# Hybrid attention and DeltaNet layer on one core: inverse's transposed copy moved to VectorE, beginning reordered

## The chip, the cores and the metric

The kernel runs on one core of one Trainium2 chip. The metric is the device time of one execution in microseconds (us). Less is better. The kernel before took 1398.04 us as the median of 3 runs (1397.48 to 1400.84).

## What is computed

One layer of a hybrid decoder, in fp32, for a prompt of 512 tokens and a sample group of 8 sequences with one token each (520 token columns), width 2048. After an RMSNorm, one input projection gives all columns of two mixers, and one output projection (2048 x 2048) ends the layer, with a second RMSNorm and the residual.

```python
h = rmsnorm(x, g_pre); p = h @ w_in          # 8208 columns: q,k,v,z of A; q,k,v of B, z of B; beta, a
# mixer A: 8 heads x 128, dilated windows (128,1), (512,4), (2048,16), partial rotary on 32 dims
# mixer B: gated DeltaNet, 8 heads x 128; conv of width 4, SiLU, l2 norms, chunks
a_mat = where(strict, (kbeta @ k.T) * decay, 0)
t_mat = triangular_solve(a_mat + eye, eye)   # the inverse U of this text, per chunk and head
u = t_mat @ (v * beta);  w = t_mat @ (kbeta * exp(gcum))
# then a recurrence over the chunks with a 128x128 state per head
y = x + rmsnorm(concat(o_a * silu(z_a), o_b * silu(z_b)) @ w_out, g_post)
```

The caches, the conv rows and the states are outputs too. The kernel uses chunks of 128 tokens where the reference has 64; the result is the same.

## The kernel before, in words

The five engines run hand-written streams that meet in semaphores. The activations are kept transposed (model dimension on the partitions, tokens on the free axis) and every projection operand is split into a high part (`h_hi`, `w_hi`) and a remainder (`h_lo`, `w_lo`), both fp32r, so that three matmuls at fp32r speed stand for one fp32 product. For each output tile of 128 columns, 16 blocks of the model dimension times 3 matmuls are needed, for each of two halves of the 520 tokens (`HALF` = 260): 96 matmuls in 8 *segments* of 12 (`segment`, L521 to L539, the matmuls on L532 to L534; a segment is one half and one quarter q of the model dimension). Each half has a PSUM bank of `PJ`.

**Tiles.** Tile T = 0 holds the 16 columns of beta and a (`w_ba`), tiles 1 to 64 the 8 columns groups of each of the 8 heads, then 16 tiles of the output projection. SP loads the weights of tile T + 1 in four quarters, ScalarE copies each to `w_hi` (`hi`, L885), VectorE and GpSimd form `w_lo` (L1266, L1733), all while TensorE works on tile T.

**The order of the other work.** All work of the two mixers is woven into the projection: each engine has generators (`own_b`, `own_a`, `mix_b`, `delta_decode`, `tail_a`, `attn_decode`, `gates`), and `step(work)` advances each of them to its next `yield` after every segment. So a head's stretch of 8 tiles has 64 steps, and which operation stands behind which in an engine's queue follows from the steps and from the order of the generators in the list: `own_a` stands ahead of `mix_b`, and `mix_b` ahead of `delta_decode`.

**The inverse.** `mix_b` forms for each chunk of 128 tokens the inverse U (`b_U`) of a unit triangular matrix by doubling. There are 7 levels; at level n the blocks of size 2^n are joined. GpSimd multiplies the matrix by a mask for the level (L1786) and makes the first U (L1791). For n = 1 to 6: TensorE multiplies the mask's block by the transposed copy T (`b_T`) (Y, L705), ScalarE copies Y to SBUF (L1135), TensorE multiplies Y by U (Z, L715) and, for n = 1 to 5, U by Y (L720); VectorE subtracts Z from U (L1492) and L720's product from T (L1495) and clears part of Y (L1496). The first T is made by four transposes on TensorE (L694) and a copy on ScalarE (L1131). Between L705 and L715, and between L720 and the next L705, TensorE runs one segment:

```python
for n in range(1, LEVELS):
    yield
    ...
    pe.wait_ge(s["mix_UT"], UTS * h + 3 * (n - 1) - 1)
```

In the same steps VectorE has the rope of mixer A (`rope_on`, L1353 to L1355) and the additions into the decode state (L1578, behind TensorE's outer product L775), the two small operations L1570 and L1571 ahead of them.

**The beginning.** SP loads the samples, chunk 0 of the prompt, the norm's weights, the identity, chunk 1, small state rows, chunks 2 and 3, the 16 columns of small weights, constants, then tile 1. ScalarE squares each chunk (L961) and takes the inverse root (L890, L891), VectorE scales (`x_scale`, L1292), TensorE transposes (state rows L556, samples L560, chunks L571), ScalarE and VectorE split into high and low (`x_hi` L969, `x_lo` L1299). When all 4 chunks and the samples are split, TensorE starts tile 0.

Of the kernel before, what the change touches and what calls it, by code (L numbers as in the profile page):

```python
# [12 lines left out]
P = 128  # L13
# [4 lines left out]
HALF = TT // 2  # L18
# [49 lines left out]
def layout(x):  # L68
# [5 lines left out]
         "w_ba": w[:, 64 * P:].reshape(NQ, 4, P, 16).transpose(0, 2, 1, 3),  # L74
# [9 lines left out]
class Chain:  # L84
# [73 lines left out]
def build(nc, x_prompt, x_sample, cache_k, cache_v, state_conv, state_delta, g_pre, w_in, w_ba, conv_w, a_log, dt_bias,  # L158
# [7 lines left out]
    with ExitStack() as ctx:  # L166
# [43 lines left out]
        s_in = sz[:, 0:P]  # L210
        xba = cq[0:16, :]
# [30 lines left out]
        vecT = sb("vecT", [P, KT + 1])  # L242
# [41 lines left out]

        def all_blocks(x, n, odd):
            return x.rearrange("p c (k a s) -> p (c k) a s", a=2, s=1 << n)[:, :, odd, :]

        def mx(n):
# [4 lines left out]
            "c_in g_in consts s_loaded x_sq rstd_ok x_scaled hT_ps h_hi_ok h_lo_ok st_ps st_sb memset_ok "  # L293
# [13 lines left out]
            "mix_kk mix_qk mix_A mix_QK mix_B mix_U0 mix_T_ps mix_T mix_Y_ps mix_Y mix_Z mix_UT ch_kS ch_r "  # L307
# [26 lines left out]
        def _(sp):  # L334
# [16 lines left out]
            sp.dma_start(xin[:, 1, :], x_prompt[0, P:2 * P, :]).then_inc(x_in[1], 16)  # L351
            sp.dma_start(scin[0:24], state_conv[0].rearrange("b i c -> (b i) c")).then_inc(s["c_in"], 16)
# [3 lines left out]
            for c in range(2, NC):  # L356
                sp.dma_start(xin[:, c, :], x_prompt[0, c * P:(c + 1) * P, :]).then_inc(x_in[c], 16)
# [14 lines left out]
            for q in range(NQ):  # L372
                wait_lo(0, q)
                load_w(w_in, tile_of(0, 0), q)
            sp.wait_ge(s["x_sq"], NC + 1)
# [145 lines left out]
        def _(pe):  # L521
            def segment(T, par, half, q, first=False):
# [3 lines left out]
                if q == 0 and not first:  # L526
                    pe.wait_ge(s["proj_sb"], 2 * T - 1 + half)
                tok = slice(half * HALF, (half + 1) * HALF)
                out = PJ[:, half, 0:HALF]
# [16 lines left out]
            def stretch(h, work):  # L546
                for j in range(NT):
                    project(NT * h + (T_H + j), (1 + j) % 2, work)
                over(work)


            pe.wait_ge(s["c_in"], 80)
            pe.transpose(MD[:, 0, 0:KT + 1], s_in[0:KT + 1], ident[0:KT + 1, 0:KT + 1]).then_inc(s["st_ps"], 1)
            for m in range(3 * NH):
                bank, o = m // 12, (m % 12) * 28
# [1309 lines left out]
```

## Time and profile before

| what | value |
|---|---|
| median of 3 runs | 1398.04 us |
| profiled execution, its own time | 1396.91 us |
| span of the profile | 1395.1 us |
| mean granted TensorE clock | 0.975 of full speed |
| TensorE busy | 1313.8 us (94%) |
| VectorE, ScalarE, GpSimd busy | 785.9, 535.7, 338.4 us |

The profile shows one execution, taken by the hardware profiler; an engine's row gives start, duration, source line, operation, operands and, in brackets, how long the engine sat idle before it and who released it. PEld is TensorE's weight load. Matmuls are pipelined, so the durations of neighbours overlap; the distance of their starts is what one costs.

### The profile page before, as it was taken

To read this page: it belongs to the slowest core of one execution; us is meant where nothing else is said; L and a number is where in the kernel's file an instruction comes from. 1 tells how busy PE (TensorE), PEld (TensorE's weight loads), DVE (VectorE), ACT (ScalarE), POOL (GpSimd) and SP (SyncE) were. 2 spreads that over 40 slices of the span, in tenths; PEclk is the share of its full clock that TensorE was granted. 3 is DMA by queue.
4 is the path that set the end of the run, shared out by engine and by line. 5 is a ranking of instruction groups with operands and counts; after the bars stand their busy time and mean duration, and the time that the engine had idled before them with its cause. 6 is when DMAs were issued, how large, how long until landed. Compare 5 with 4: busy or idle time off the path is not lost.

```text
span 1395.1 us, 29226 instructions
## 1 busy us (share of the span) xinstructions
PE 1313.8 (94%) x10446; PEld 1265.7 (91%) x10446; DVE 785.9 (56%) x1873; ACT 535.7 (38%) x1447; POOL 338.4 (24%) x287
## 2 busy tenths in 40 slices
PE   4999999999999999999999899989998998989997
PEld 3998998999899988998999899989998997989996
DVE  6366366636763676367636763676267635474445
ACT  6243346224633363246323633363236325512210
POOL 0224212421242124212421242124212411212220
PEclk9999999999999999999999999999999999989999
DMA  5332324233423342324133423342334233422253
GB/s 185 114 104 72 107 87 152 71 99 95 152 71 94 100 152 71 96 98 152 71 94 100 152 71 92 102 147 76 91 103 156 81 107 133 144 70 89 94 184 126
DMA packets 84638, 151.81 MB, mean 109 GB/s; under 512 B 10873, under 2 KB 29266, under 8 KB 82962
## 3 DMA queue, kind: packets, MB, share of 16 engines
q1 hardware_dynamic: 74158, 144.87, 32.3%
q10 hardware_dynamic: 10384, 5.50, 1.4%
q8 instruction: 81, 1.33, 0.4%
q14 instruction: 15, 0.12, 0.0%
HBM read 132.19 MB, written 17.27 MB: 107 GB/s over the span
## 4 chain that ended last, share of the span: by engine, by line
PE 69%; DVE 15%; issue 7%; ACT 6%; DMA 1%; POOL 1%; ACTq 0%; SPq 0%; DVEq 0%; POOLq 0%
PE PJ L532 15%; PE PJ L533 15%; PE PJ L534 15%; PE MX L705 3%; PE MX L715 2%; DVE memx L1416 2%; PE MX L720 2%; DVE memx L1427 2%; ACT kv L1183 1%; PE MD L757 1%; ACT w_hi L885 1%; PE MX L637 1%; PE MX L617 1%; DVE kv L1592 1%; PE MD L775 1%
## 5 line engine op out<-in xcount | busy, mean ns | idle before, releaser
L532 PE MATMUL PJ<-h_hi,w_hi 128*128 128x260 f32 x2432 | 725.4, 298 | 3.0 <-DVE w_lo L1266 1.6
L533 PE MATMUL PJ<-h_lo,w_hi 128*128 128x260 f32 x2432 | 694.4, 286 | 0.0
L534 PE MATMUL PJ<-h_hi,w_lo 128*128 128x260 f32 x2432 | 692.9, 285 | 0.0
L532 PEld LDWEIGHTS PJ<-h_hi,w_hi 128*128 128x128 f32 x2432 | 466.2, 192 | 21.1 <-issue 8.9
L533 PEld LDWEIGHTS PJ<-h_lo,w_hi 128*128 128x128 f32 x2432 | 465.9, 192 | 2.8 <-issue 1.7
L534 PEld LDWEIGHTS PJ<-h_hi,w_lo 128*128 128x128 f32 x2432 | 465.2, 191 | 0.0
L1733 POOL TENSOR_TENSOR w_lo<-w_raw,w_hi 128x512 fp32r<-128x512 f32 (+1 forms) x162 | 214.2, 1322 | 941.4 <-ACT w_hi L885 941.4
L885 ACT ACTIVATE w_hi<-w_raw 128x512 fp32r<-128x512 f32 (+1 forms) x324 | 199.0, 619 | 103.9 <-PE PJ L534 81.1
L1266 DVE TENSOR_TENSOR w_lo<-w_raw,w_hi 128x512 fp32r<-128x512 f32 (+1 forms) x162 | 116.1, 723 | 164.8 <-ACT w_hi L885 160.1
L1135 ACT ACTIVATE mem<-MX 128x256 f32<-128x256 f32 x48 | 18.6, 389 | 215.3 <-PE MX L705 215.3
L1786 POOL TENSOR_TENSOR mem<-mem,levels 128x512 f32<-128x512 f32 x56 | 71.8, 1293 | 33.8 <-DVE mem L1474 33.8
L1492 DVE TENSOR_TENSOR mem<-mem,MX 128x256 f32<-128x256 f32 x48 | 20.1, 418 | 85.5 <-PE MX L720 72.3
L1416 DVE SCALAR_TENSOR_TENSOR memx<-memx,cw 128x512 f32<-128x512 f32 x72 | 60.8, 844 | 1.7
L912 ACT ACTIVATE memx<-PJ 128x260 f32<-128x260 f32 (+1 forms) x130 | 49.4, 380 | 23.3 <-PE PJ L534 20.9
L818 PE MATMUL PJ<-h_hi,w_hi 128*128 128x260 f32 x160 | 50.1, 313 | 7.1 <-DVE h_lo L1642 3.0
L705 PE MATMUL MX<-mem 128*128 128x64 f32 x384 | 48.8, 270 | 6.8 <-DVE mem L1495 6.8
L705 PEld LDWEIGHTS MX<-mem 128*128 128x128 f32 x384 | 46.9, 191 | 8.4 <-DVE mem L1495 7.3
L1592 DVE CUSTOM_DVE_ANT_0 kv<-kv,qb 128x128 f32<-128x128 f32 x192 | 52.2, 329 | 0.0
L715 PE MATMUL MX<-mem 128*128 128x64 f32 x384 | 48.0, 268 | 0.0
L819 PE MATMUL PJ<-h_lo,w_hi 128*128 128x260 f32 x160 | 47.3, 295 | 0.0
L820 PE MATMUL PJ<-h_hi,w_lo 128*128 128x260 f32 x160 | 47.1, 295 | 0.0
L715 PEld LDWEIGHTS MX<-mem 128*128 128x128 f32 x384 | 47.0, 191 | 0.0
(306 smaller groups left out, 1671.3 us busy)
## 6 DMA issues: line engine op xcount, KB each, us to landing
w_raw<-in_w_in SPq DMA_DIRECT2D x256, 256.0 KB, 2.6
w_raw<-in_w_out SPq DMA_DIRECT2D x64, 256.0 KB, 2.8
kv<-in_cache_win_k SPq DMA_DIRECT2D x24, 512.0 KB, 3.4
kv<-in_cache_win_v SPq DMA_DIRECT2D x16, 512.0 KB, 4.1
mem<-in_x_prompt SPq DMA_DIRECT2D x4, 1024.0 KB, 10.9
S<-in_state_delta SPq DMA_DIRECT2D x8, 512.0 KB, 3.4
out<-S SPq DMA_DIRECT2D x8, 512.0 KB, 3.8
out<-mem ACTq DMA_DIRECT2D x16, 256.0 KB, 2.3
```

What stands on the lines that cost most here:

```text
L532: pe.matmul(out, wh, h_hi[:, k, tok], start=k == 0, stop=False)
L533: pe.matmul(out, wh, h_lo[:, k, tok], start=False, stop=False)
L534: last = pe.matmul(out, wl, h_hi[:, k, tok], start=False, stop=k == KT - 1)
L705: last = pe.matmul(blocks(mx(1)[:, c, :], n, 0), b_B[n % 2][:, c, :], blocks(b_T[:, c, :], n, 0), start=True, stop=True)
L715: last = pe.matmul(blocks(mx(2)[:, c, :], n, 1), b_Y[:, c, :], blocks(b_U[:, c, :], n, 1), start=True, stop=True)
L818: pe.matmul(out, wh, h_hi[:, k, tok], start=start and i == 0, stop=False)
L885: act.activation(w_hi[:, par, 4 * q:4 * q + 4, 0:n], w_raw[:, q, :, 0:n], ACT.Copy).then_inc(s["w_hi_ok"], 1)
L1266: dve.tensor_tensor(w_lo[:, par, 4 * q:4 * q + 4, 0:n], w_raw[:, q, :, 0:n], w_hi[:, par, 4 * q:4 * q + 4, 0:n].bitcast(F32), ALU.subtract ...
L1416: link(dve.scalar_tensor_tensor(acc[:, 0:TP], xq[:, i:i + TP], w[:, 24 + i:25 + i], acc[:, 0:TP], ALU.mult, ALU.add))
L1592: last = dve.tensor_tensor_reduce(out=x, in0=x, in1=qb[:, b * HD:(b + 1) * HD], scale=1.0, scalar=0.0, op0=ALU.mult, op1=ALU.add, accum_ou ...
L1733: pool.tensor_tensor(w_lo[:, par, 4 * q:4 * q + 4, 0:n], w_raw[:, q, :, 0:n], w_hi[:, par, 4 * q:4 * q + 4, 0:n].bitcast(F32), ALU.subtrac ...
L1786: ins = pool.tensor_tensor(b_B[n % 2], b_A, levels[:, n, :].unsqueeze(1).to_broadcast((P, NC, P)), ALU.mult)
```

## The change

1. *Transposed copy.* TensorE's first transposes (L694), ScalarE's copy (L1131) and, at levels 1 to 4, L720 and L1495 are gone. VectorE instead transposes U as a whole, 128x512, in blocks of 32x32, once behind U's making (in the step of L1482) and once behind each L1492 of the levels 1 to 4. At level 5 L720 and L1495 stay.
2. *Halves.* The two token halves are 256 and 264 columns wide instead of 260 and 260, in all tiles.
3. *Beginning.* The DMAs are issued in another order, the small weights come in one load with another layout, tile 1's weights ahead of chunks 2 and 3, the samples and the state rows behind them. The first half (chunks 0 and 1) of tiles 0 and 1 is projected first, with the transposes of the constants, of chunk 2, of the samples and of chunk 3 between the segments, then the second half of both. The samples are scaled by the norm's weights behind their transposes instead of ahead.

```diff
-HALF = TT // 2
+SPLIT = 2 * (TP // 4)
+TOKENS = (slice(0, SPLIT), slice(SPLIT, TT))
+WIDTH = (SPLIT, TT - SPLIT)
+def bank(T, half):
+    return T if isinstance(T, int) and T < 2 else half
+def made(T, half):
+    return 2 * half + T + 1 if isinstance(T, int) and T < 2 else 2 * T + half + 1
...
@@ sync: order of the loads @@
-            sp.dma_start(xs_in, x_sample.rearrange("b t d -> (b t) d")).then_inc(x_in[NC], 16)
-            sp.dma_start(xin[:, 0, :], x_prompt[0, 0:P, :]).then_inc(x_in[0], 16)
             for n in range(2):
                 sp.dma_start(g_bc[n], g_pre[0, n * WA:(n + 1) * WA].partition_broadcast(P)).then_inc(s["g_in"], 16)
-            sp.dma_start(ident[:], c_ident).then_inc(s["c_in"], 16)
+            sp.dma_start(xin[:, 0, :], x_prompt[0, 0:P, :]).then_inc(x_in[0], 16)
+            sp.dma_start(ident[:], c_ident).then_inc(s["ba_in"], 16)
+            sp.dma_start(ba_raw, w_ba).then_inc(s["ba_in"], 16)
             sp.dma_start(xin[:, 1, :], x_prompt[0, P:2 * P, :]).then_inc(x_in[1], 16)
+            for q in range(NQ):
+                load_w(w_in, tile_of(0, 0), q)
+            for c in range(2, NC):
+                sp.dma_start(xin[:, c, :], x_prompt[0, c * P:(c + 1) * P, :]).then_inc(x_in[c], 16)
+            sp.dma_start(xs_in, x_sample.rearrange("b t d -> (b t) d")).then_inc(x_in[NC], 16)
...
-            for q in range(NQ):
-                sp.dma_start(w_raw[:, q, :, 0:16], w_ba[q]).then_inc(raw_in[q], 16)
...
@@ tensor @@
+            def first_tiles():
+                after = {(0, 1): const_transposes, (0, 3): lambda: x_transposes(2), (1, 1): sample_transposes,
+                         (1, 3): lambda: x_transposes(3)}
+                for half in range(2):
+                    for T in range(2):
+                        for q in range(NQ):
+                            if half == 1 and T == 0:
+                                pe.wait_ge(s["h_lo_ok"], 4 * NC - 3 + q + 1)
+                            elif T == 0:
+                                pe.wait_ge(s["h_lo_ok"], 4 + q + 1)
...
+                            if half == 0 and (T, q) in after:
+                                after[T, q]()
...
-                pe.wait_ge(s["mix_U0"], h + 1)
-                for c in chunks:
-                    last = pe.transpose(mx(0)[:, c, :], b_U[:, c, :], ident[:])
-                last.then_inc(s["mix_T_ps"], 1)
...
-                    if n < LEVELS - 1:
+                    if n == LEVELS - 2:
                         for c in chunks:
                             last = pe.matmul(blocks(mx(3)[:, c, :], n, 0), b_U[:, c, :],
                                              blocks(b_Y[:, c, :], n, 0), start=True, stop=True)
...
@@ scalar: the beginning, and the copy @@
+            x_rstd(0, 0)
+            x_rstd(1, 1)
+            ba_hi()
+            x_rstd(2, 2)
+            x_hi(0)
+            x_hi(1)
+            x_rstd(3, 3)
+            for q in range(NQ):
+                hi(1, 1, q, first=True)
+            x_rstd(4, NC)
...
-                act.wait_ge(s["mix_T_ps"], h + 1)
-                act.activation(b_T, mx(0), ACT.Copy).then_inc(s["mix_T"], 1)
...
@@ vector: mix_b @@
                 dve.tensor_tensor(sz, xz, ez, ALU.mult).then_inc(s["z_ok_b"], 1)
+                dve.wait_ge(s["mix_U0"], h + 1)
+                dve.transpose(flat(b_T), flat(b_U)).then_inc(s["mix_T"], 1)
                 yield
                 for n in range(1, LEVELS):
                     yield
                     yield
-                    z = (2 * LEVELS - 3) * h + 2 * (n - 1) + 1
-                    dve.wait_ge(s["mix_Z"], z)
-                    if n < LEVELS - 1:
-                        dve.wait_ge(s["mix_Z"], z + 1)
+                    dve.wait_ge(s["mix_Z"], LEVELS * h + n + n // (LEVELS - 2))
                     u = all_blocks(b_U, n, 1)
                     dve.tensor_tensor(u, u, all_blocks(mx(2), n, 1), ALU.subtract).then_inc(s["mix_UT"], 1)
-                    if n < LEVELS - 1:
+                    if n < LEVELS - 2:
+                        dve.wait_ge(s["mix_UT"], UTS * h + 3 * n - 2)
+                        dve.transpose(flat(b_T), flat(b_U)).then_inc(s["mix_UT"], 1)
+                    elif n == LEVELS - 2:
                         t = all_blocks(b_T, n, 0)
                         dve.tensor_tensor(t, t, all_blocks(mx(3), n, 0), ALU.subtract).then_inc(s["mix_UT"], 1)
```

## Rows read from the trace of the kernel before

**Rows 1.** The page, busy time by engine and the chain that ended last.
```profile
PE 1313.8 (94%) x10446; PEld 1265.7 (91%) x10446; DVE 785.9 (56%) x1873; ACT 535.7 (38%) x1447; POOL 338.4 (24%) x287
...
PE 69%; DVE 15%; issue 7%; ACT 6%; DMA 1%; POOL 1%; ACTq 0%; SPq 0%; DVEq 0%; POOLq 0%
```

**Rows 2.** TensorE by line: count, busy us, mean ns of one, idle before.
```profile
L720 PE MATMUL MX<-mem 128*128 128x64 f32 x320 | 42.3, 275 | 0.0
...
L694 PE MATMUL MX<-ident,mem 128*128 128x128 f32 x32 | 4.9, 276 | 1.4 <-POOL mem L1791 1.4
```

**Rows 3.** Timeline of TensorE, third head: start us, us, what, idle before.
```profile
400.22 0.60 PE L694 MATMUL MX<-ident,mem 128*128 128x128 f32 x4
...
405.63 1.00 PE L715 MATMUL MX<-mem 128*128 128x64 f32 x8
406.46 1.06 PE L720 MATMUL MX<-mem 128*128 128x64 f32 x8
...
408.86 1.00 PE L705 MATMUL MX<-mem 128*128 128x64 f32 x8
409.79 1.12 PE L775 MATMUL MD<-rb 8*128 8x512 f32 x2
...
416.59 1.10 PE L705 MATMUL MX<-mem 128*128 128x64 f32 x8 [0.83 <-DVE mem L1495]
```

**Rows 4.** Timeline of VectorE, the same stretch.
```profile
400.10 1.00 DVE L1571 SCALAR_TENSOR_TENSOR gS<-dd,vecT,memx 128x8 f32 x1
...
407.56 0.42 DVE L1492 TENSOR_TENSOR mem<-mem,MX 128x256 f32<-128x256 f32 x1 [1.60 <-PE MX L720]
...
411.55 1.16 DVE L1353 TENSOR_TENSOR memx<-memx,memr 32x520 f32<-32x520 f32 x1
...
414.32 1.56 DVE L1355 TENSOR_TENSOR memx<-memx,memr 32x520 f32<-32x520 f32 x1
415.81 0.40 DVE L1492 TENSOR_TENSOR mem<-mem,MX 128x256 f32<-128x256 f32 x1
...
433.01 0.62 DVE L1353 TENSOR_TENSOR memx<-memx,memr 32x520 f32<-32x520 f32 x1
```

**Rows 5.** Timeline of GpSimd, the same stretch.
```profile
399.92 1.16 POOL L1786 TENSOR_TENSOR mem<-mem,levels 128x512 f32<-128x512 f32 x1
...
412.12 3.20 POOL L1786 TENSOR_TENSOR mem<-mem,levels 128x512 f32<-128x512 f32 x2
...
425.51 2.29 POOL L1786 TENSOR_TENSOR mem<-mem,levels 128x512 f32<-128x512 f32 x2
```

**Rows 6.** TensorE waits: releaser, total us, times, longest.
```profile
PE MX L705 <- DVE mem L1495: 6.8, 8, 0.9
```

**Rows 7.** Beginning: timelines of ScalarE, VectorE and TensorE.
```profile
17.50 1.91 ACT L961 ACTIVATE memr<-mem 128x2048 f32<-128x2048 f32 x1 [2.19 <-DMA mem<-in_x_prompt]
...
26.66 2.04 ACT L969 ACTIVATE h_hi<-MX 128x512 fp32r<-128x512 f32 x4
...
21.87 0.69 DVE L1299 TENSOR_TENSOR h_lo<-MX,h_hi 128x512 fp32r<-128x512 f32 x1 [0.65 <-ACT h_hi L969]
...
15.75 2.74 PE L556 MATMUL MX<-ident,memx 28*128 28x28 f32 x24
...
37.81 0.56 PE L532 MATMUL PJ<-h_hi,w_hi 128*128 128x260 f32 x1 [1.64 <-DVE w_lo L1266]
...
41.10 0.28 PE L532 MATMUL PJ<-h_hi,w_hi 128*128 128x260 f32 x1
41.22 0.28 PE L533 MATMUL PJ<-h_lo,w_hi 128*128 128x260 f32 x1
```

**Rows 8.** Windows: length, busy us (instructions) of PE, PEld, DVE, ACT, POOL; PEclk, DMA share, GB/s.
```profile
30.00:40.00 10.00, 5.91 (x31) 5.00 (x31) 7.66 (x12) 4.09 (x11) 0.60 (x2) 0.71 0.08 29
386.00:393.00 7.00, 7.00 (x35) 7.00 (x35) 6.83 (x12) 2.16 (x7) 3.13 (x2) 0.53 0.08 23
525.00:532.00 7.00, 7.00 (x62) 7.00 (x62) 6.47 (x12) 2.40 (x8) 3.29 (x2) 1.00 0.11 35
```

More of the change, by code:

```diff
@@ L544, in project, with stretch, x_transposes @@
                         step(work)
-            def stretch(h, work):
-                for j in range(NT):
+            def stretch(h, work, first=0):
+                for _ in range(SEGS * first):
+                    step(work)
+                for j in range(first, NT):
                     project(NT * h + (T_H + j), (1 + j) % 2, work)
                 over(work)
[L552 to L555, printed above, removed]
-                pe.transpose(MX[:, 2 + bank, o:o + 28], scin[:, m * P:(m + 1) * P], ident[0:28, 0:28]).then_inc(
-                    s["st_ps"], 1)
-            pe.wait_ge(s["x_scaled"], 2)
-            for k in range(KT):
-                last = pe.transpose(MD[:, 1, k * NB:(k + 1) * NB], xs_in[:, k * P:(k + 1) * P], ident[0:NB, 0:NB])
-            last.then_inc(s["hT_ps"], 1)
-            for c in range(NC):
+            def x_transposes(c):
                 for b in range(4):
                     if b % 2 == 0:
-                        pe.wait_ge(s["x_scaled"], 2 * c + 2 + b // 2 + 1)
+                        pe.wait_ge(s["x_scaled"], 2 * c + b // 2 + 1)
                     if c > 0:
-                        pe.wait_ge(s["h_lo_ok"], 4 * (c - 1) + b + 2)
-                    elif b == 2:
-                        pe.wait_ge(s["st_sb"], 2)
+                        pe.wait_ge(s["h_lo_ok"], 4 * (c - 1) + b + 1)
                     for k in range(4):
@@ L798, in attn_decode @@
                 last.then_inc(s["pv_ps"], 1)
-            pe.wait_ge(s["consts"], 80)
             pe.wait_ge(s["memset_ok"], 1)
-            project(0, 0, [], first=True)
-            stretch(0, [gates(), own_b(0), own_a(0), mix_b(0), delta_decode(0)])
+            first_tiles()
+            stretch(0, [gates(), own_b(0), own_a(0), mix_b(0), delta_decode(0)], first=1)
             with repeat(pe, 1, NH) as h:
@@ L875, in _, with hi @@
             ch = Chain(act, s["act_chain"])
-            def hi(T, par, q, n=P, first=False):
-                act.wait_ge(raw_in[q], 16 * T + 16)
+            def hi(T, par, q, first=False):
+                act.wait_ge(raw_in[q], 16 * T)
                 if not first:
@@ L942, in stretch @@
                     for seg in range(SEGS):
+                        if isinstance(h, int) and h == 0 and j == 0:
+                            if seg == 0:
+                                copy_out(0, 0, xba)
+                                guard(0, 0)
+                                copy_out(1, 0, *DST[0])
+                            elif seg == 6:
+                                copy_out(0, 1, xba)
+                            step(work)
+                            if seg % 2 == 0:
+                                hi(2, 0, seg // 2)
+                            continue
                         if seg == 0:
@@ L977, in _ @@
+            x_hi(1)
+            x_rstd(3, 3)
+            for q in range(NQ):
+                hi(1, 1, q, first=True)
+            x_rstd(4, NC)
+            act.wait_ge(s["rstd_ok"], NC + 1)
+            act.activation(xs_in, xs_in, ACT.Copy, scale=rstd[0:NB, NC:NC + 1]).then_inc(s["rstd_ok"], 1)
+            act.wait_ge(s["st_ps"], 3 * NH + 1)
+            act.activation(vecT[:], MD[:, 0, 336:336 + 2 * KT + 1], ACT.Copy).then_inc(s["st_sb"], 1)
             for m in range(2):
-                act.wait_ge(s["st_ps"], 12 * m + 13)
@@ L985, in _ @@
-            x_rstd(NC, NC - 1)
-            x_hi(1)
             x_hi(2)
+            act.wait_ge(s["x_scaled"], 2 * NC + 1)
+            act.activation(h_hi[:, :, TP:TT], xs_T, ACT.Copy).then_inc(s["h_hi_ok"], 1)
             x_hi(3)
-            act.wait_ge(s["memset_ok"], 1)
-            for q in range(NQ):
-                hi(0, 0, q, 16, first=True)
             def gates():
@@ L1186, in attn_decode @@
                     last.then_inc(s["prod"], 1)
-            for seg in range(SEGS):
-                if seg % 2 == 0:
-                    hi(1, 1, seg // 2, first=True)
-                if seg == 4:
-                    copy_out(0, 0, xba)
-            stretch(0, (xba, 0), [gates(), own_b(0), own_a(0), mix_b(0), delta_decode(0)])
+            stretch(0, None, [gates(), own_b(0), own_a(0), mix_b(0), delta_decode(0)])
             ch.end(1)
```

168 lines of the change are left out of this document (98 added, 70 removed).

## The prediction

> **What bounds the kernel now.** I read the page's busy times first: TensorE is busy 94% of the span, VectorE 56%, and the chain that ended last runs through TensorE for 69% of it [rows 1]. So a matmul taken away from TensorE is worth its full time wherever TensorE doesn't then wait for someone. The list by line gives the groups that the change takes away: L720, the product that updates the transposed inverse, has 320 records (8 heads x 5 levels x 4 chunks, two records each), and L694, the first transposes, 32 [rows 2]. TensorE's timeline of the third head shows the pace: product L715 starts at 405.63, L720 at 406.46, and the next level's L705 at 408.86 [rows 3]. VectorE's timeline shows what stands between two levels (a subtraction into U at 407.56, one into the transposed copy behind it), and that at 411.55 the rope work of head mixer A comes in between [rows 4]; GpSimd's shows its multiplications by the level masks [rows 5]. The waits name one place where VectorE holds TensorE in this ladder: L705 behind L1495, 8 times, 0.9 us at most [rows 6]. For the beginning I read the three engines' timelines [rows 7], and for the clock some windows [rows 8].
>
> **What the change takes from TensorE.** In the levels 1 to 4 of every head L720 goes; level 5 keeps it, since blocks of 32 that lie off the diagonal are not reached by a transpose of 32x32 blocks. A group's 8 records have a mean of 275 ns but overlap: the group runs from 406.46 to 407.52, and the first record behind it comes in 8 pitches of 0.11, 0.89 us after its start (by the same pitch L694's four take 0.44 us) [rows 2, 3]. Per head 4 x 0.89 + 0.44 = 4.0 us, for 8 heads 32.0; with L694 the 1.4 us go that TensorE waited there for GpSimd's U [rows 2]. Together **33.4 us**. ScalarE loses one copy per head; it isn't on the path there, so that counts nothing.
>
> **What it puts on VectorE.** Per head five transposes of 128x512 fp32, in the place of four subtractions of 0.41 us. No transpose on VectorE is in the trace. The nearest row with 512 elements is an fp32 subtraction of 128x512, 0.69 us [rows 7]; I take X = 0.70 for the transpose. The lower bound is 0.41, what it replaces (256 elements). The upper bound I take from the longest row with that much data, 1.56 us, a subtraction that shares its time with GpSimd [rows 4]; I can't exclude a slower one, and that is a rival. Does 0.70 hide? VectorE now waits only for L715 (its last record ends when L720 would have run for about 0.17 us), then subtracts from PSUM, waits for itself, and transposes. TensorE runs one projection segment meanwhile: 12 matmuls at a pitch of 0.12 us, 1.44 us [rows 7]. From the end of the issue of L715: VectorE starts 0.2 later (407.56 behind 407.35 [rows 3, 4]), needs 0.42 for U, 0.04 to go on, X, and 0.04 to wake TensorE; TensorE is back after 1.53 (the same distance as 406.46 + 0.89 + 1.53 = 408.88, where L705 stands [rows 3]). That is X + 0.7 against 1.5: the wait is X - 0.80, so nothing at 0.70, with 0.1 us to spare. The levels 1, 3 and 4 cost nothing.
>
> At **level 2** it doesn't hide. There the three rope operations stand ahead in VectorE's queue. The first starts at 411.55, behind work that waits for L775 (409.79), and the last ends at 415.88; U's subtraction follows at 415.81, and TensorE gets L705 at 416.59 after 0.83 us of waiting [rows 3, 4]. L775 comes 0.44 + 0.89 = 1.33 earlier after the change, and the rope operations with it, and so does GpSimd, whose multiplications make them long (two of them in 3.20 us at 412.12 [rows 5]; the same rope operation without company takes 0.62, here 1.16 [rows 4]). So U is ready at 415.81 - 1.33 + 0.40 = 414.88, the transpose at 415.62, L705 at 415.66. TensorE alone would be there at 416.59 - 0.83 - 2.22 = 413.54. Its wait is 2.12 instead of 0.83: **1.29 us more per head, 10.3 in all**. What is late next is nothing further, since level 3 starts from L705.
>
> The **first transpose** waits in VectorE's queue for GpSimd's U, ready when GpSimd goes on at 399.92 [rows 5]. Behind it are queued the two small operations of the delta-rule decode, the last of which ran from 400.10 to 401.10 [rows 4]. The transpose ends at about 400.7, so they end near 402.2; L775's first group needs them at about 402.6. Level 1's L705 needs the transpose at about 401.7. Cover 0.4 and 1.0 us: cost 0, and 0.4 per head (3 us) if the order on the shared engines falls badly.
>
> Heads: 33.4 - 10.3 = **23.1 us**.
>
> **The beginning.** Before, the first projection matmul starts at 37.81 and then 2 x 96 run, T0 and T1 [rows 7]. After, the first 256 tokens of both tiles come first, so TensorE can start when chunks 0 and 1 are split. ScalarE's order is now chunk 0, chunk 1, small weights, the squares of chunk 2, and only then the split of chunk 0: so **the landing of chunk 2** is the gate. Before, it was there at 17.50 [rows 7], behind 4.46 MB issued up to it; after, it stands behind 5.19 MB (a weight tile of 1 MB comes ahead, the state rows go behind), at 15.5 us for 4.46 MB (the first data move some 2 us in) that is 2.5 us later: 20.0. The squares and the two small operations take about 2.5, so the split begins at 22.5. ScalarE needs 0.5 to 0.6 for a block and VectorE 0.69 for its low part [rows 7]; four blocks of chunk 0 and the first of chunk 1: 22.5 + 0.6 + 5 x 0.69 = 26.5. Then 192 matmuls x 0.12 = 23.0, as before, and work that lay in TensorE's idle time and is now between the segments: 25 constant transposes 2.8 (2.74 for 24 [rows 7]), 16 sample and 32 chunk transposes at 0.11, 5.3. Start of tile T2, at full clock: 26.5 + 23.0 + 8.1 = 57.6 against 37.8 + 23.0 = 60.8. SP's queue loses four loads of the small weights with 64-byte pieces; nothing waits for the constants behind them, so 0. The clock was at 0.71 of full speed in 30 to 40 [rows 8], and either order has a cold stretch; I count it equal, with up to 1.5 us more after. **3.2 us**, between 0 and 6.
>
> **Halves of 256 and 264** instead of 260 and 260: at full clock the pitch is 0.12 us where 260 columns at 2.4 GHz are 0.108, so something beside the columns counts. With a linear dependence the two halves cancel: 0. All 7,776 projection matmuls are touched, so each ns of the mean pitch is 7.8 us; I see no row for a step at 256.
>
> **Sum.** The profiled execution took 1396.9 (span 1395.1); minus 23.1 minus 3.2 gives 1370.6. The runs' median is 1398.0, 1.1 above it, so 1371 to 1372.
>
> **Rivals.** (A) *The transpose is slow, and VectorE becomes the ladder's bound.* Only X decides. The extra wait over the sum is 8 x 3 x (X - 0.80) + 8 x (X - 0.70). At half an element per cycle (X about 1.2) that is 13.6: **1385**. The gain of 26.3 is gone at X = 1.60 us; at 2.3 us (a quarter) the loss is 49 and the time **1420**, slower. For it: VectorE has no row of that kind, and the slack is only 0.1 us. Against it: one-input operations with 512 fp32 elements all stand near 0.6 to 0.7.
>
> The Trainium skill, "VectorE: DVE Perf Modes", section "The three transpose paths", gives 311 ns for 128x128 bf16 on VectorE; with 384 more elements at one per cycle of 0.96 GHz the estimate for 512 is 0.71 us, if fp32 goes at the same rate. No run here shows it yet.
>
> (B) *The transposes and GpSimd's multiplications exclude each other*, as the rope operation does (1.16 against 0.62 [rows 4]). At level 4 the multiplication at 425.51 (two in 2.29 us [rows 5]) falls on the transpose. A wait of half to a whole of 1.15 us, less 0.1, is 0.5 to 1.05 per head, 4 to 8 us: **1375 to 1380**. The Trainium skill, "SBUF — State Buffer", section "SBUF: two separate sides", says that an exclusive lock is taken by a VectorE operation with two SBUF inputs or in a mode with two ports against GpSimd. By that rule the rope rows agree (they have two inputs), and a one-input transpose would be free unless it runs in the two-port mode.
>
> (C) *The clock decides.* In 386 to 393 it is at 0.53 and 35 matmuls run, in 525 to 532, the same stage of the next head, at 1.00 and 62 [rows 8]. So a fall costs up to 27 x 0.12 = 3.2 us, and which heads have it depends on how the heads lie against it. Two heads more or less: 6 us either way, **1365 or 1378**. A pitch that falls by 1 ns with the new halves gives 1363.
>
> **Numbers.** My forecast (1364 to 1378) has 0.58; (A) at half rate or (B) 0.22; (A) beyond X = 1.5 0.10; below 1364 by (C), the pitch or a milder level 2 0.10. The range 1357 to 1386 takes in the first two and most of the last. A measurement tells 0.3%, 4.2 us, from no change. Faster 0.89, same 0.03, slower 0.08.
>
> **What would show it.** VectorE rows of the transpose near 0.70; L720 with 64 records, L694 gone; L705's wait about 2.1 us per head in one place; tile T2 at about 58 to 60; heads 2.9 us shorter. A transpose over 0.8 with waits at every level, or a mean pitch of the projection away from 0.12, proves the sum wrong.

## The result and the profile after

The kernel after took **1415.61 us** (median of 4 runs, 1412.15 to 1417.73), the kernel before on the same chip 1397.76 (4 runs, 1395.43 to 1400.84). The ratio is **1.0124, with an interval of 1.0094 to 1.0154**: the change made the kernel slower by 18 us, where 26 us less were forecast. The profiled execution of after took 1412.15 us, with a span of 1410.3 and a mean granted clock of 0.956; before it was 1396.91, 1395.1 and 0.975.

The names of lines moved. L705, L715 and L720 of before are L746, L756 and L761; L775 is L816; L1492 and L1495 are L1553 and L1559; L1570 and L1571 are L1635 and L1636; L1786, L1791, L1809 and L1733 are L1849, L1854, L1872 and L1796. The first transpose is L1546, those of the levels are L1556.

The page of after, busy times and chain, beside [rows 1]:

```profile
PE 1304.8 (93%) x10158; PEld 1254.3 (89%) x10158; DVE 814.6 (58%) x1880; ACT 532.6 (38%) x1440; POOL 340.9 (24%) x287
...
PE 62%; DVE 17%; issue 9%; ACT 7%; POOL 3%; DMA 1%; SPq 0%; ACTq 0%; DVEq 0%; POOLq 0%
```

TensorE has 288 instructions and 9 us of busy time less, VectorE 29 us more. The work was taken away as planned, and still the span grew by 15.2 us, so time went into waits and into slower matmuls. The waits of TensorE in after (releaser, total us, times, longest), beside [rows 6]:

```profile
PE MX L746 <- DVE mem L1556: 17.2, 8, 2.2
PE MD L816 <- DVE gS L1636: 16.8, 8, 2.3
PE MX L710 <- DVE memx L1508: 14.3, 7, 2.1
...
PE MX L746 <- POOL mem L1849: 1.4, 4, 0.4
```

The first is the wait that the prediction had: 17.2 us, 2.15 per head, forecast 2.12. The third was there before (L665, 14.2 us). **The second is new**, and as large as the first: L816 waits 2.1 us per head for the result of L1636, an operation on 128x8 elements. TensorE's timeline of the third head, beside [rows 3]:

```profile
399.03 1.11 PE L746 MATMUL MX<-mem 128*128 128x64 f32 x8 [0.37 <-POOL mem L1849]
402.48 2.04 PE L816 MATMUL MD<-rb 8*128 8x512 f32 x2 [2.34 <-DVE gS L1636]
...
407.17 1.66 PE L756 MATMUL MX<-mem 128*128 128x64 f32 x8
...
418.34 1.58 PE L746 MATMUL MX<-mem 128*128 128x64 f32 x8 [2.16 <-DVE mem L1556]
```

L816 came 2.34 us late, and L746 of level 2 2.16 us late. VectorE's timeline of the same stretch, beside [rows 4]:

```profile
397.88 0.71 DVE L1546 STREAM_TRANSPOSE mem<-mem 128x512 f32<-128x512 f32 x1 [1.18 <-POOL mem L1854]
398.52 0.48 DVE L1635 TENSOR_TENSOR dd<-dd 128x8 f32<-128x8 f32 x1
399.12 3.21 DVE L1636 SCALAR_TENSOR_TENSOR gS<-dd,vecT,memx 128x8 f32 x1
...
417.57 0.71 DVE L1556 STREAM_TRANSPOSE mem<-mem 128x512 f32<-128x512 f32 x1
...
428.63 0.71 DVE L1556 STREAM_TRANSPOSE mem<-mem 128x512 f32<-128x512 f32 x1
```

The transpose of 128x512 takes 0.71 us. Behind the first one stands L1636, recorded with 3.21 us, where the same operation took 1.00 in before [rows 4]. GpSimd's timeline, beside [rows 5], has the company:

```profile
397.81 1.16 POOL L1849 TENSOR_TENSOR mem<-mem,levels 128x512 f32<-128x512 f32 x1
398.94 1.03 POOL L1872 TENSOR_TENSOR rb<-rb,ident 8x512 f32<-8x512 f32 x1
399.93 1.26 POOL L1796 TENSOR_TENSOR w_lo<-w_raw,w_hi 128x512 fp32r<-128x512 f32 x1
401.16 1.14 POOL L1849 TENSOR_TENSOR mem<-mem,levels 128x512 f32<-128x512 f32 x1
...
428.03 2.28 POOL L1849 TENSOR_TENSOR mem<-mem,levels 128x512 f32<-128x512 f32 x2
```

L1636 starts at 399.12, inside GpSimd's L1872 (to 399.97). It isn't done when that ends, nor at the end of L1796 (401.19), and ends at 402.33, 0.03 us after L1849 (402.30). In before the same operation was over 0.02 us after the first GpSimd operation that it met (399.92 + 1.16 = 401.08, L1571's end 401.10 [rows 4, 5]). The last row shows GpSimd's pair at level 4: with the transpose of 428.63 inside it, it took 2.28 us, 2.29 before [rows 5].

Windows of after around the two waits (length; busy us and instructions of PE, PEld, DVE, ACT, POOL; clock, DMA share, GB/s):

```profile
399.00:406.00 7.00, 4.63 (x17) 3.02 (x18) 4.66 (x3) 0.90 (x2) 4.33 (x4) 0.69 0.15 47
414.00:421.00 7.00, 4.84 (x33) 4.64 (x32) 4.45 (x6) 1.04 (x3) 2.66 (x2) 0.84 0.11 37
```

and the same work in the trace of before:

```profile
401.00:408.00 7.00, 7.00 (x54) 6.17 (x53) 2.32 (x5) 1.63 (x4) 4.41 (x5) 1.00 0.30 76
412.00:419.00 7.00, 6.17 (x53) 5.96 (x52) 4.79 (x7) 1.18 (x3) 3.32 (x3) 1.00 0.12 40
```

In before the clock is full in both. In after it is at 0.69 and 0.84: the level of 1.2 GHz was granted for part of each window, in or behind the stretch in which TensorE stood still. (The clock in a fall is 0.5 of full speed, so 0.69 and 0.84 are mixtures.) The stretches at half clock come from the record of the clock in each trace (nearly the same follows from the mean granted clock, as 2 x (1 - clock) x span). Over the third head the trace of after has the half clock three times, from 377.8, 401.7 and 418.8 (3.4, 6.8 and 3.4 us long); before has it once, from 385.7 (6.8 us). Over the whole kernel the stretches at half clock sum to 72.8 us before and **126.6 after**. The pitch of a projection matmul (the mean distance of the starts of two neighbours) is 0.217 us at half clock and 0.12 at full, so each such us does some 0.55 us of work and costs about 0.45; the sums below use 0.44.

Where the falls stand: between 200 and 850 us of after TensorE has 15 waits of 1.9 to 2.3 us (L710, L816 and L746 in each of five heads), and the clock falls 15 times, each time 1.6 to 8.1 us behind the start of one of these waits. The waits of 0.4 to 0.9 us have no fall of their own. In before the same stretch has 5 waits of 2.0 us (L665) and 5 falls: two behind the first wait, none behind the third, one behind each of the others.

The half-clock times below are each of a kernel's one profiled execution. By the mean clock of every execution they are 124 to 139 us in after (4 executions) and 56 to 81 in before (43 of them), so a difference of 10 us between two kernels says little.

The beginning, ScalarE's and TensorE's timeline, beside [rows 7]:

```profile
17.48 1.91 ACT L1013 ACTIVATE memr<-mem 128x2048 f32<-128x2048 f32 x1 [2.11 <-DMA mem<-in_x_prompt]
...
24.60 0.56 PE L549 MATMUL PJ<-h_hi,w_hi 128*128 128x256 f32 x1
```

Chunk 2 has landed at 17.48, and the first projection matmul starts at 24.60 instead of 37.81. Tile T2 starts at 56.5, before at 62.3: 5.8 us earlier.

These rows make a ledger, after minus before, in us of span: removed from TensorE -33.4 (worked out in the prediction); L746's wait 17.2 - 6.8 = +10.4; L816's wait +16.8; half clock (126.6 - 72.8) x 0.44 = +23.7; beginning -5.8. That makes +11.7 of +15.2. Of the other 3.5, the waits of TensorE name 2.1: the 1.4 us of waiting for GpSimd at L694, counted in the 33.4 as gone, are there again as L746's wait for the mask of level 1 (1.4 us), and L803 waits 1.4 us where before L762 waited 0.7. Some 1.4 us have no name.

### The profile page after: what moved, and what is told of

It reads as the page before. It is cut to its first block, busy times and chain, and to the rows that moved or that the text cites. A ratio compares the mean times of both kernels' runs of the same rounds, so it can differ in the third digit from the quotient of the medians.

```text
span 1410.3 us, 28604 instructions
## 1 busy us (share of the span) xinstructions
PE 1304.8 (93%) x10158; PEld 1254.3 (89%) x10158; DVE 814.6 (58%) x1880; ACT 532.6 (38%) x1440; POOL 340.9 (24%) x287
## 4 chain that ended last, share of the span: by engine, by line
PE 62%; DVE 17%; issue 9%; ACT 7%; POOL 3%; DMA 1%; SPq 0%; ACTq 0%; DVEq 0%; POOLq 0%
PE PJ L549 14%; PE PJ L550 13%; PE PJ L551 13%; PE MX L756 3%; PE MX L746 3%; DVE memx L1478 2%; DVE gS L1636 2%; DVE memx L1489 2%; ACT w_hi L925 2%; PE MD L816 1%; ACT kv L1241 1%; PE MX L682 1%; DVE kv L1657 1%; PE MX L662 1%; PE MD L798 1%
## 5 line engine op out<-in xcount | busy, mean ns | idle before, releaser
L549 PE MATMUL PJ<-h_hi,w_hi 128*128 128x264 f32 (+1 forms) x2432 | 731.7, 301 | 2.8 <-issue 1.6
L550 PE MATMUL PJ<-h_lo,w_hi 128*128 128x264 f32 (+1 forms) x2432 | 698.8, 287 | 0.0
L551 PE MATMUL PJ<-h_hi,w_lo 128*128 128x264 f32 (+1 forms) x2432 | 696.6, 286 | 0.0
L1796 POOL TENSOR_TENSOR w_lo<-w_raw,w_hi 128x512 fp32r<-128x512 f32 x160 | 213.7, 1336 | 941.5 <-ACT w_hi L925 941.5
L925 ACT ACTIVATE w_hi<-w_raw 128x512 fp32r<-128x512 f32 x320 | 198.1, 623 | 103.5 <-PE PJ L551 83.2
L1319 DVE TENSOR_TENSOR w_lo<-w_raw,w_hi 128x512 fp32r<-128x512 f32 x160 | 114.4, 720 | 148.4 <-ACT w_hi L925 144.7
L1849 POOL TENSOR_TENSOR mem<-mem,levels 128x512 f32<-128x512 f32 x56 | 71.5, 1289 | 33.1 <-DVE mem L1536 33.1
L746 PE MATMUL MX<-mem 128*128 128x64 f32 x384 | 52.6, 282 | 18.6 <-DVE mem L1556 17.2
L1553 DVE TENSOR_TENSOR mem<-mem,MX 128x256 f32<-128x256 f32 x48 | 20.1, 418 | 84.2 <-PE MX L756 71.6
L746 PEld LDWEIGHTS MX<-mem 128*128 128x128 f32 x384 | 48.5, 198 | 21.4 <-DVE mem L1556 16.4
L952 ACT ACTIVATE memx<-PJ 128x264 f32<-128x264 f32 (+2 forms) x130 | 49.3, 380 | 27.5 <-PE PJ L551 25.0
L756 PE MATMUL MX<-mem 128*128 128x64 f32 x384 | 56.4, 298 | 0.0
L756 PEld LDWEIGHTS MX<-mem 128*128 128x128 f32 x384 | 56.3, 224 | 0.0
L858 PE MATMUL PJ<-h_hi,w_hi 128*128 128x256 f32 (+1 forms) x160 | 49.6, 310 | 7.0 <-DVE h_lo L1705 2.9
L859 PE MATMUL PJ<-h_lo,w_hi 128*128 128x256 f32 (+1 forms) x160 | 46.9, 293 | 0.0
```

The costliest lines, as they stand in the source:

```text
L549: pe.matmul(out, wh, h_hi[:, k, tok], start=k == 0, stop=False)
L550: pe.matmul(out, wh, h_lo[:, k, tok], start=False, stop=False)
L551: last = pe.matmul(out, wl, h_hi[:, k, tok], start=False, stop=k == KT - 1)
L746: last = pe.matmul(blocks(mx(1)[:, c, :], n, 0), b_B[n % 2][:, c, :], blocks(b_T[:, c, :], n, 0), start=True, stop=True)
L756: last = pe.matmul(blocks(mx(2)[:, c, :], n, 1), b_Y[:, c, :], blocks(b_U[:, c, :], n, 1), start=True, stop=True)
L858: pe.matmul(out, wh, h_hi[:, k, tok], start=start and i == 0, stop=False)
```

## The experiments

**Two theories** stood first. **Q**: the new wait at L816 comes from where the first transpose stands, ahead of the two small operations, so that the second of them starts amid GpSimd's work; and the waits bring the falls of the clock. **K**: the falls come with the missing matmuls of L720, wherever the waits are. Under N, where an expectation names it, the cost lies in neither, so that taking the waits away moves little. Each kernel was run beside the kernel before on the same chip (its medians there 1395.28 to 1397.52).

**e1: the first transpose behind the two small operations.** One step later in VectorE's list, nothing left out:

```diff
-                dve.wait_ge(s["mix_U0"], h + 1)
-                dve.transpose(flat(b_T), flat(b_U)).then_inc(s["mix_T"], 1)
                 yield
                 for n in range(1, LEVELS):
                     yield
+                    if n == 1:
+                        dve.wait_ge(s["mix_U0"], h + 1)
+                        dve.transpose(flat(b_T), flat(b_U)).then_inc(s["mix_T"], 1)
                     yield
```

> The changed kernel with VectorE's first transpose of each head moved one step later, behind the two small operations of the delta-rule decode (L1635, L1636). Theory Q (queue and lock): the transpose held L1636 back until it fell on four GpSimd operations in a row (3.21 us instead of 1.0), and the outer product L816 waited 2.1 us per head for it; such waits also bring the falls of the clock. Expected: L1636 back to about 1.0 us, L816's wait under 0.3 us per head, L746's wait at level 2 still 2.1 us, half-clock time down from 127 us to about 90 to 100, time 1388 to 1400 us. Rival K (the falls of the clock come from the matmuls that are gone, not from waits): the wait goes, the half-clock time stays at 120 to 130 us, time about 1400 us or above. Rival N (other causes in the heads): 1410 us or above.

Measured 1387.57 us, ratio 0.9931 (0.991 to 0.9952), 0.4 us under the expected range. In its waits and by its source line (count: least/median/most ns):

```profile
PE MX L746 <- DVE mem L1557: 17.2, 8, 2.2
...
L1637 DVE SCALAR_TENSOR_TENSOR gS<-dd,vecT,memx x8: 1000/1002/1090, 112.0 to 1086.4; 128x8 f32 x7, 128x8 f32<-128x8 f32 x1
```

L816 no longer waits for VectorE, the small operation is back at 1.00 us, and level 2's wait stays as it was. Half-clock time fell from 126.6 to 100.4 us. By the ledger, -16.8 (wait) and 26.2 x 0.44 = -11.5 (clock) make -28.3; the spans differ by -27.4. One operation moved by one step was worth 28 us (1415.61 to 1387.57), and turns slower into faster.

**e2: the same wait removed from GpSimd's side.** The order on VectorE stays; GpSimd waits for the small operation's result before it starts L1872:

```diff
                 yield from idle(3)
+                pool.wait_ge(s["gated_bd"], h + 1)
                 for n in range(2):
                     pool.wait_ge(s["d_rows_ok"], h + 1)
```

> The changed kernel with one wait more on GpSimd: its first expansion of v for the outer product (L1872 of the changed kernel) waits until L1636 on VectorE is done. The order on VectorE stays. Theory Q: L1636 has no GpSimd operation beside it any more and takes about 0.2 us instead of 3.21, L816's wait goes (under 0.5 us per head), time 1388 to 1400 us. If GpSimd is not what makes L1636 long, it stays at 3.2 us, GpSimd and TensorE come later still, and the time is 1415 us or above. Rival K on the clock as for the first kernel.

Measured 1388.65 us, ratio 0.9942 (0.9925 to 0.9958).

```profile
L1636 DVE SCALAR_TENSOR_TENSOR gS<-dd,vecT,memx x8: 226/228/230, 112.9 to 1087.8; 128x8 f32 x7, 128x8 f32<-128x8 f32 x1
```

Without GpSimd beside it the same 128x8 operation takes **0.228 us**, against 1.0 and 3.2. The wait is gone and half-clock time is 100.4, as in e1. So it isn't the transpose's 0.71 us of length that cost 2 us, but the company in which it left the operation behind it.

**e3: the rope operations behind the inverse's in VectorE's list.** The first transpose stays where after has it:

```diff
-                stretch(h, [tail_a(h - 1), attn_decode(h - 1), own_b(h), own_a(h), mix_b(h), delta_decode(h)])
+                stretch(h, [tail_a(h - 1), attn_decode(h - 1), own_b(h), mix_b(h), own_a(h), delta_decode(h)])
```

> The changed kernel with mixer A's rope placed behind the inverse's work in VectorE's list of generators, so that at level 2 the subtraction and the transpose come ahead of the three rope operations. Theory Q: L746's wait (2.15 us per head at level 2) goes to under 0.3 us, L816's wait of 2.1 us stays, time down by 17 us for the waits alone and by up to 13 us more if falls of the clock go with it: 1385 to 1399 us. Rival K: 1398 to 1400 us with the half-clock time unchanged. If the rope only moves its wait to the next level: 1410 us or above.

Measured 1381.52 us, ratio 0.9894 (0.9868 to 0.9919), 3.5 us under the expected range. L746's wait is gone, L816's isn't:

```profile
PE MD L816 <- DVE gS L1636: 16.4, 8, 2.3
```

Half-clock time 110.1 us, 16.5 less than in after. The 17.2 us of wait and 7.3 of clock make 24.5; the spans differ by 29.9.

**e4: e1 and e3 together**, both edits as above, nothing else.

> The changed kernel with both edits, the first transpose a step later and the rope behind the inverse. Theory Q: neither wait is left, the falls of the clock go back to about one per head (half-clock time about 75 us), time 1356 to 1372 us, below both kernels. Rival K: only the two waits go, 8 x 4.3 = 34 us, the half-clock time stays above 115 us, time 1378 to 1385 us.

Measured **1359.85 us, ratio 0.9736 (0.972 to 0.9752)**. The waits that it still has at L710, as every kernel, and in the ladder, three of 1.1 us for GpSimd:

```profile
PE MX L710 <- DVE memx L1508: 14.4, 7, 2.1
...
PE MX L746 <- POOL mem L1850: 3.2, 3, 1.1
```

Half-clock time is 75.2 us, close to before (72.8), with all the L720 of levels 1 to 4 gone; by the mean clock the four executions have 73 to 84. That speaks against K, which had 1378 to 1385 here.

**e5: e2 and e3 together**, both edits as above.

> The changed kernel with the rope behind the inverse and GpSimd waiting for L1636 (instead of the later transpose). Both waits should be gone as in the fourth kernel (1359.9 us). GpSimd's level masks come later by its wait, so TensorE may wait for them: 1355 to 1370 us. A step above 1375 would say that holding GpSimd back costs a wait of its own.

Measured 1359.17 us, ratio 0.973 (0.9707 to 0.9752); half-clock time 78.2. The two cures of L816's wait are worth the same.

**e6 and e7: the parts alone.** e6 has the new beginning and the new halves with the old inverse; the ladder's edits of after are put back:

```diff
+                pe.wait_ge(s["mix_U0"], h + 1)
+                for c in chunks:
+                    last = pe.transpose(mx(0)[:, c, :], b_U[:, c, :], ident[:])
+                last.then_inc(s["mix_T_ps"], 1)
...
-                    if n == LEVELS - 2:
+                    if n < LEVELS - 1:
...
-                dve.wait_ge(s["mix_U0"], h + 1)
-                dve.transpose(flat(b_T), flat(b_U)).then_inc(s["mix_T"], 1)
```

> The beginning and the halves of 256 and 264 of the changed kernel alone; the inverse as before (TensorE's transposes and L720 at all levels, no transpose on VectorE). The changed kernel's trace has the second tile's start 5.8 us earlier than before and the mean pitches of the two halves cancel (0.1183 and 0.1209 us), so 1397.5 - 6 = 1391.5 us, 1388 to 1394. If the new beginning or the halves bear part of the slowdown, 1398 us or above.

Measured 1390.45 us, ratio 0.9959 (0.9947 to 0.9971).

e7 is the kernel before with the new inverse alone, the same places the other way round:

```diff
-                pe.wait_ge(s["mix_U0"], h + 1)
-                for c in chunks:
-                    last = pe.transpose(mx(0)[:, c, :], b_U[:, c, :], ident[:])
-                last.then_inc(s["mix_T_ps"], 1)
...
-                    if n < LEVELS - 1:
+                    if n == LEVELS - 2:
...
+                dve.wait_ge(s["mix_U0"], h + 1)
+                dve.transpose(flat(b_T), flat(b_U)).then_inc(s["mix_T"], 1)
```

> The new inverse alone, in the kernel before (beginning and halves as before). Theory Q: the heads carry the whole loss, so 1415.6 + 6 = 1421.6 us, 1417 to 1426. If the loss needs both parts, below 1410 us.

Measured 1423.54 us, ratio 1.0178 (1.0148 to 1.0207).

```profile
PE MD L774 <- DVE gS L1571: 16.5, 8, 2.4
...
PE MX L704 <- DVE mem L1491: 14.9, 7, 2.2
```

It has the same two waits (16.5 us for the small operation, 14.9 at level 2) and the longest half-clock time of all kernels, 147.0 us. The beginning and the halves give 7 us; the inverse takes 26.

**e8: the kernel before, with the first transpose added and nothing removed.** It writes into a tile of its own that nobody reads:

```diff
+        spare = sb("spare", [P, TP])
...
                 dve.tensor_tensor(sz, xz, ez, ALU.mult).then_inc(s["z_ok_b"], 1)
+                dve.wait_ge(s["mix_U0"], h + 1)
+                dve.transpose(spare[:], flat(b_U))
```

> The kernel before with one thing added and nothing removed: VectorE transposes U once per head, in the place where the change puts it, into a spare tile that nobody reads. All matmuls stay. Theory Q: the queue position alone makes the wait: L1571 takes about 3.2 us instead of 1.0, the outer product L775 waits 1.5 to 2 us per head (12 to 16 us), and falls of the clock are added though no matmul is gone: half-clock time up from 73 us by 25 us or more, time 1412 to 1428 us. Rival K (falls come from missing matmuls): half-clock time stays near 73 us, time 1409 to 1413 us. If the removed matmuls were what made room for the wait: no wait, time 1398 us.

Measured **1434.22 us, ratio 1.0261 (1.0237 to 1.0284)**, 6 us above the expected range. Its waits of TensorE, and VectorE's groups (count, busy us, mean ns, idle before):

```profile
PE MD L779 <- DVE gS L1577: 12.2, 8, 1.6
...
L1577 DVE SCALAR_TENSOR_TENSOR gS<-dd,vecT,memx 128x8 f32 (+1 forms) x8 | 25.8, 3220 | 0.9
...
L1488 DVE STREAM_TRANSPOSE spare<-mem 128x512 f32<-128x512 f32 x8 | 5.7, 711 | 9.4 <-POOL mem L1797 9.4
```

Eight transposes of 5.7 us in all, on an engine that is busy 56% of the time, cost 37 us. All the products of L720 are there, so K can't explain it. TensorE waits 12.2 us more, and half-clock time grows from 72.8 to 131.4: 12.2 + 58.6 x 0.44 = 38.0, and the spans differ by 37.8. My expectation was low because it counted too little for the clock.

**e9: the kernel before, with only the rope work moved** (the edit of e3).

> The kernel before with nothing but the rope placed behind the inverse in VectorE's list: how much of the gain of the third to fifth kernel is the order's alone. Its wait of L705 (6.8 us in 8 heads) goes: 1396.5 - 6.8 = 1389.7 us, 1385 to 1391 with what falls of the clock go with it. If the order matters only where the transposes are, 1395 us or above.

Measured 1392.44 us, ratio 0.9967 (0.9953 to 0.998), a little above the expected range. The 6.8 us of L705's wait are gone; half-clock time is 82.7, 9.9 more than before. The span fell by 6.1 where wait and clock together say 6.8 - 4.4 = 2.4, so the ledger can be off by some 4 us on a single kernel. The reordering alone was worth little, since before had only 0.83 us per head there.

**e10 and e12: the wait of L710** (14.1 to 14.7 us in every kernel, under this or another line number). L710 waits for L1508 on VectorE. e10 is e5 with the inverse's mixer first in VectorE's list:

```diff
-                stretch(h, [tail_a(h - 1), attn_decode(h - 1), own_b(h), mix_b(h), own_a(h), delta_decode(h)])
+                stretch(h, [mix_b(h), tail_a(h - 1), attn_decode(h - 1), own_b(h), own_a(h), delta_decode(h)])
```

> The fifth kernel (rope behind the inverse, GpSimd waits; 1359.2 us) with the inverse's generator first in VectorE's list, so that the product that makes q (L1508) no longer stands behind the decode's additions (L1682, L1685). Theory Q, applied to another place: TensorE's wait at L710 (14.3 us, 2.0 in each of 7 heads) goes, and as waits bring the falls of the clock and the fall after L710 comes in most heads, part of those falls too: 1359 - 14 - (0 to 10) = 1335 to 1345 us. Rival K (the clock does not follow the waits): 1345 us with the half-clock time near 78 us. If the additions then hold up the decode's product (L837), no gain: 1357 to 1361 us.

Measured 1360.82 us, ratio 0.9741 (0.9715 to 0.9768): a miss. The wait is 14.3 us still, and the long operation L1685 still stands directly ahead of L1508. My guess was that it belongs to the step before and not to the same one. e12 is e10 with L1685 one step later:

```diff
-                yield from idle(1)
+                yield from idle(2)
                 dve.wait_ge(s["prod"], 3 * hh + 3)
                 dve.tensor_tensor(V_TILE[0], V_TILE[0], V_TILE[2], ALU.add).then_inc(s["pv_sum"], 1)
-                yield from idle(4)
+                yield from idle(3)
```

> The tenth kernel with the second addition of the sampled values (L1685) moved one step later on VectorE, so that it stands behind L1508 (in the tenth it stood one step ahead, and the new list order changed nothing). Theory Q: L1508 starts about 2 us earlier, L710's wait (14.3 us) goes, falls of the clock with it: 1360.8 - 14 - (0 to 12) = 1335 to 1347 us. Rival K: 1346 us with the half-clock time unchanged at 80 to 97 us. If the addition then makes L837 wait: above 1355 us.

Measured 1360.15 us, ratio 0.9725 (0.9686 to 0.9765): a miss again. VectorE's timeline in e12:

```profile
359.16 2.11 DVE L1685 TENSOR_TENSOR kv<-kv,qb 128x1024 f32<-128x1024 f32 x1
361.19 0.69 DVE L1508 TENSOR_TENSOR memx<-memx 128x520 f32<-128x520 f32 x1
```

L1685 still stands directly ahead of L1508, so neither edit changed the order that it was meant to change, and the guess behind e12 isn't borne out. The two runs test neither theory. The wait is 14.4 us; how to remove it stays open. GpSimd has a part in it: L1685 takes 2.10 to 2.11 us in seven heads, where it starts inside GpSimd's L1796, and 1.22 in the last, where it has no company.

**e11: e5 with every transpose of levels 1 to 4 made twice**, the first of each pair into a spare tile.

```diff
                         dve.wait_ge(s["mix_UT"], UTS * h + 3 * n - 2)
+                        dve.transpose(spare[:], flat(b_U))
                         dve.transpose(flat(b_T), flat(b_U)).then_inc(s["mix_UT"], 1)
```

> The fifth kernel with the transpose of levels 1 to 4 made twice, once into a spare tile (nobody reads it): the ladder's slack measured. By the prediction's sum a transpose hides until 0.80 us; two take 0.71 + 0.61 = 1.32, so a wait of 0.5 us at each of 4 levels in 8 heads: L746's wait 16 to 18 us, time 1359 + 17 = 1376 us, and up to 12 more if small waits also bring falls of the clock: 1373 to 1390 us. If there was more slack than the sum says: under 1370 us.

Measured 1384.98 us, ratio 0.9913 (0.9889 to 0.9936), inside the expected range.

```profile
PE MX L747 <- DVE mem L1558: 12.6, 32, 0.5
```

The pair takes 1.30 us (the second starts 0.64 behind the first and lasts 0.67), and TensorE waits 12.6 / 32 = 0.39 us per level. The rule of the prediction, X - 0.80, gives 0.50; the slack is thus 0.91. Half-clock time went from 78.2 to 106.7: 12.6 + 28.5 x 0.44 = 25.1, and the spans differ by 26.2. So each us of wait cost two (25.8 us in all).

## Why the prediction was wrong

**Right.** The bound of the kernel, and the removal: e5, with the new inverse and without the two waits, stands 31.3 us below e6 with the old one (1390.45 - 1359.17). The prediction's 33.4 and the 6.8 of L705's wait make 40.2. The profiled execution of e5 has 19.4 us more at half clock than that of e6 (78.2 against 58.8), 8.5 us of time, and that leaves 31.7 where the two spans differ by 28.1: the sum is some 4 us too high. X: all 40 transposes took 0.71 us, forecast 0.70. This is after's source line of the 32 at the levels (least/median/most ns, first and last time):

```profile
L1556 DVE STREAM_TRANSPOSE mem<-mem x32: 711/712/714, 122.7 to 1144.6; 128x512 f32<-128x512 f32 x32
```

Level 2: 2.15 us of wait per head, forecast 2.12, by the mechanism given (three rope operations ahead in the queue); e3 takes the operations away and the wait goes. The halves: at full clock the pitch is 0.1183 us for 256 columns and 0.1209 for 264, on average 0.1196, against 0.1197 for 260: nothing, as forecast.

**Wrong, the first step**: "The first transpose ... so they end near 402.2; L775's first group needs them at about 402.6 ... Cover 0.4 and 1.0 us: cost 0". The sum moved the end of the two small operations by 1.1 us (401.10 to 402.2) and kept the 1.00 us that the second showed in before. But that 1.00 us is itself a wait for GpSimd: the operation alone takes 0.23 (e2). Moved by 1.1 us (it starts at 401.2 in before's time, not at 400.10), it met another GpSimd operation and took 3.21. It ended 0.03 us behind a GpSimd operation; in before's time (the third head of after lies 2.1 us earlier) the end is at 404.4 and not 402.2, where 402.6 was the need. The 3 us that I allowed "if the order on the shared engines falls badly" were 16.8. The Trainium skill, "SBUF — State Buffer", section "SBUF: two separate sides", says that a VectorE operation with two SBUF inputs and a GpSimd operation exclude each other for whole instructions. The trace agrees for this operation (0.23 alone, 3.21 in company), and it shows that the wait can last past the ends of two GpSimd operations.

**Wrong, the second step**: "I count it equal", of the clock, and rival C, which took the falls for a matter of luck, 3.2 us for a head. They go with the waits: 53.8 us more at half clock in after, 23.7 us of time, and only 2.4 us more at half clock than before once the waits are gone (e4; over all executions the medians are 67 us in before, 129 in after and 82 in e4). So even the wait that was forecast right had the wrong price: to take away level 2's 17.2 us gained 28 us from e1 to e4 and 34 from after to e3.

**Mis-sized**: the slack of a level, 0.91 us instead of 0.80 (e11); without effect, since 0.71 is below both. The beginning, 5.8 us instead of 3.2: chunk 2 landed at 17.48 and not at 20.0, as the 0.73 MB more ahead of it cost it nothing. Of the 2.6 us more, 1.1 lies in after (T2 at 56.5, forecast 57.6) and 1.5 in before (62.3, where the sum, at full clock, had 60.8): before runs the first 3.1 us of its projection at half clock, after the first 1.6, so the clock wasn't equal there either. In e6 beginning and halves together are 7 us.

**The rivals.** (A) falls: X is 0.71. (B) falls as put: the transpose at 428.63 lies inside GpSimd's pair and neither is longer (0.71; 2.28 against 2.29). The exclusion was the right mechanism at the wrong place: it doesn't take the transpose but the two-input operation behind it. That the transpose has one input doesn't by itself explain why it is spared: L1619, a 128x8 multiplication of one tensor by a constant, takes 0.16 us with GpSimd at rest and 1.25 in the four heads of after in which it starts inside L1796. (C) holds in its prices but not in its cause. The case that came, a two-input operation pushed into GpSimd's company, was none of the cases, and the 0.08 on slower was for another mechanism.

**What stays open.** Why L1636 loses at two ends of GpSimd operations, when in before and in e1 it gets in at the first: the runs show both and not the reason. In all eight heads of after the end at which it is done is the one behind which GpSimd rests, as GpSimd's next operation waits for L816, which waits for L1636 (2.30 us in the third head); so no run shows how long it would wait with more work queued there. Rest isn't needed in general (in before GpSimd goes on at once), and an end of L1796 can let VectorE in: L1619 is done 0.03 us behind one, with the next GpSimd operation already begun. That the waits lower the clock rests on where the falls stand and on nine kernels (after, e1 to e5, e7, e8, e11) in which half-clock time rises and falls with them; the sizes don't follow strictly. e9 has one wait less than before and 9.9 us more at half clock; e10 has 96.5 us at half clock and e12 79.5 with the same waits and the same time within 1 us, but the four executions of e10 alone go from 79 to 95. What decides whether a wait of 2 us brings a fall of 3.4 or of 6.8 us, or none, isn't shown.

**The best version** is e4, e5, e10 or e12, which can't be told apart (1359.2 to 1360.8 us, 2.6 to 2.7% below before): the change, with the transpose behind the small operations or GpSimd held back for them, and the rope work behind the inverse.

## What to carry to other kernels

Ahead of an insertion on an engine with idle time, look at each operation queued behind it, and compare its duration with one of the same kind elsewhere: a 128x8 operation of 1.00 us is already a wait for a neighbour, and took 3.2 here when it was moved by 1.1. Price an added wait of TensorE, where it is the busy engine, at more than its length: a us of wait cost 1.6 us here (e1 against after), 2 (e11) and 3 (e8), since the half clock came with it. When work is taken off the bound engine, move whatever stands ahead of the next link in the same edit: the two reorderings together were worth 56 us here (1415.61 to 1359.85), more than the matmuls removed.

## What the runs showed of the hardware

- A 128x8 VectorE operation with two inputs in SBUF took 0.228 us with GpSimd at rest, 1.00 when it got in after one GpSimd operation, and 3.21 us when passed over at two ends of such operations.
- The 32x32 block transpose of 128x512 fp32 took 0.711 us (0.711 to 0.714 over 32 in after), inside a GpSimd operation too; two in a row have a pitch of 0.64 (e11).
- A 128x8 VectorE operation with one tensor input (L1619) took 0.16 us with GpSimd at rest and 1.25 us when it started inside a GpSimd operation (after).
- Added waits of TensorE of 1.5 to 2.3 us, once or twice in a head of 140 us, went together with a growth of half-clock time from 72.8 to 126.6 us (after) and to 131.4 (e8). In after, from 200 to 850 us, each of the 15 falls began 1.6 to 8.1 us behind the start of a wait of 1.9 to 2.3 us.
- A projection matmul of 256, 260 and 264 columns has a pitch of 0.1183, 0.1197 and 0.1209 us at full clock, so without a step at 256.
